# Two weight units of the last expert moved by sixteen transfers of eight rows each

## What is computed

```
def moe_swiglu(h, router_w, w_gate, w_up, w_down):
    logits = (h @ router_w).astype(jnp.float32)
    top_val, top_idx = lax.top_k(logits, TOP_K)
    gates = jax.nn.softmax(top_val, axis=-1)
    ...
    for e in range(N_EXPERTS):
        out = out + gate_dense[..., e:e + 1] * swiglu(h, w_gate[e], w_up[e], w_down[e])
```

## Time and profile before

| | us |
|---|---|
| three runs | 1363.33, 1363.97, 1364.43 |
| their median | 1363.97 |
| the profiled execution | 1363.78 |
| its span | 1361.9 |
| TensorE busy, matmuls | 1296.3 (95%) |
| VectorE busy | 469.0 (34%) |
| ScalarE busy | 341.4 (25%) |
| TensorE waiting for expert weights | 45.3 in 40 waits |

### The profile page before, as it was taken

One profiled execution on the slowest core, in us unless ns is written; L12 is line 12 of the kernel. 1 busy time (PEld: TensorE's weight loads), 2 busy tenths in 40 slices (PEclk: granted clock), 3 DMA queues, 4 the chain that ended last, 5 costly groups with the idle time before them and its releaser, 6 DMA issues.

```text
span 1361.9 us, 31406 instructions
## 1 busy us (share of the span) xinstructions
PE 1296.3 (95%) x14058; PEld 947.3 (70%) x14058; DVE 469.0 (34%) x821; ACT 341.4 (25%) x593; POOL 85.6 (6%) x113
## 2 busy tenths in 40 slices
PE   9999999999999999999987789999999999999875
PEld 9889999999998995467552243366676677558333
DVE  7777776777786662100101101000100100110121
ACT  8666443343377552000100000000000000000011
POOL 1000000000000004101020010001001001001000
PEclk9999999999999999999999999999999999999999
DMA  9316544454433289999999999999999999999993
GB/s 372 109 61 248 208 167 182 186 186 172 170 132 106 98 363 425 413 424 414 427 423 419 427 424 418 424 425 414 428 424 415 427 425 414 426 423 421 419 422 156
DMA packets 46736, 443.91 MB, mean 326 GB/s; under 512 B 6992, under 2 KB 9168, under 8 KB 13328
## 3 DMA queue, kind: packets, MB, share of 16 engines
q1 hardware_dynamic: 40896, 434.15, 77.4%
q0 software_dynamic: 5424, 7.51, 2.0%
q10 hardware_dynamic: 288, 0.29, 0.1%
HBM read 438.20 MB, written 5.93 MB: 326 GB/s over the span
## 4 chain that ended last, share of the span: by engine, by line
PE 78%; DMA 11%; SPq 5%; DVE 3%; ACT 2%; issue 1%; another core or an unknown queue 0%; ACTq 0%; DVEq 0%
PE bank L632 77%; DMA moe_ring<-experts 10%; SPq L458 5%; DVE w_pairs L1425 1%; DMA ring<-stream 1%; PE bank L636 0%; PE bank L730 0%; DVE nmx L1510 0%; ACT scratch L1182 0%; PE bank L736 0%; ACT w_pairs L1104 0%; ACT scratch L1181 0%; ACT sq L1124 0%; ACT scratch L1179 0%; DVE parts L1439 0%
## 5 line engine op out<-in xcount | busy, mean ns | idle before, releaser
L632 PE MATMUL bank<-moe_ring,hT 128*32 128x448 f32 x5376 | 512.6, 539 | 31.0 <-DMA moe_ring<-experts 27.9
L632 PEld LDWEIGHTS bank<-moe_ring,hT 128*32 128x32 f32 x5376 | 251.3, 110 | 288.1 <-issue 181.5
L632 PE MATMUL bank<-parts,w_pairs 128*128 128x272 f32 (+1 forms) x3360 | 427.2, 289 | 1.2 <-DVE w_pairs L1432 0.5
L632 PEld LDWEIGHTS bank<-parts,w_pairs 128*128 128x128 f32 x3360 | 421.7, 188 | 4.7 <-issue 2.8
L632 PE MATMUL bank<-moe_ring,scratch 128*32 128x256 f32 x4704 | 270.9, 383 | 18.6 <-DMA moe_ring<-experts 17.3
L1773 DVE SCALAR_TENSOR_TENSOR hT<-bank,slot_norm,scratch 128x224 f32<-128x224 f32 x96 | 40.6, 423 | 705.9 <-ACT scratch L1334 705.9
L632 PEld LDWEIGHTS bank<-moe_ring,scratch 128*32 128x32 f32 x4704 | 199.8, 111 | 90.3 <-issue 23.3
L1425 DVE TENSOR_TENSOR w_pairs<-ring,w_pairs 128x2048 fp32r<-128x2048 f32 x68 | 154.5, 2287 | 32.2 <-ACT w_pairs L1104 32.1
L1334 ACT ACTIVATE scratch<-bank,norm_now 128x224 f32<-128x224 f32 x96 | 41.2, 447 | 494.7 <-PE bank L632 494.7
L1104 ACT ACTIVATE w_pairs<-ring 128x2048 fp32r<-128x2048 f32 x68 | 129.6, 1912 | 90.1 <-PE bank L632 90.0
L1344 ACT ACTIVATE scratch<-bank,slot_gate 128x256 f32<-128x256 f32 x21 | 9.2, 474 | 242.6 <-PE bank L632 242.6
(11 more groups left out here) (216 smaller groups left out, 490.8 us busy)
## 6 DMA issues: line engine op xcount, KB each, us to landing
moe_ring<-experts SPq DMA_DIRECT2D x192, 1792.0 KB, 42.7
ring<-stream SPq DMA_DIRECT2D x68, 1024.0 KB, 5.1
ring<-stream SPq DMA_DIRECT2D x4, 512.0 KB, 7.4
ring<-stream SPq DMA_DIRECT2D x2, 976.0 KB, 4.7
ring<-stream SPq DMA_DIRECT2D x2, 768.0 KB, 10.5
hT<-h SPq DMA_DIRECT2D x4, 272.0 KB, 5.1
ring<-stream SPq DMA_DIRECT2D x4, 256.0 KB, 4.7
acc_rows<-scratch POOLq DMA_DIRECT2D x1, 1024.0 KB, 5.3
```

Of the source, the lines that this page charges most:

```text
L632: return release(nc.tensor.matmul(dst, lhsT, rhs, start=start, stop=stop), inc, count)
```

## The change

A second set of semaphores is made, one for each of the two units in `SPREAD`, the 2nd and the 6th of an expert (m = 1 and 5). `load_expert` gets a flag `final`. With it, these two units are not moved by one transfer of 128 rows but by sixteen: for each block of 32 partitions and each b of 0 to 3, the eight rows a + b, a + b + 4, ..., a + b + 28. All sixteen raise the unit's own semaphore, to 256 in sum, and the buffer's usual semaphore isn't raised for this unit. Which bytes go to which partition is unchanged. The loop of SyncE over the passes is cut so that the very last pass is issued by a separate call with `final=True`; its number is read from `rounds_sb`. TensorE waits in the last pass for 256 on the new semaphore for these two units, and for the units twelve places later in the same buffers it waits for 16 less on the usual one.

```diff
--- before.py
+++ after.py
@@ -70,6 +70,7 @@
 HSLOTS = 3
 PAIR_AT = (4, 0, 2)
 BIG_UNIT = 3584
+SPREAD = (1, 5)
 MOE_SLOTS = 12
 MOE_FROM = 2048
 
@@ -294,7 +295,7 @@
         bank = [banks[:, i, :] for i in range(8)]
 
         slot_in = [sem(f"slot_in{i}") for i in range(SLOTS)]
-        moe_in = [sem(f"moe_in{i}") for i in range(MOE_SLOTS)]
+        moe_in, spread_in = [sem(f"moe_in{i}") for i in range(MOE_SLOTS)], [sem(f"spread_in{i}") for i in range(len(SPREAD))]
         direct_used, split_hi, split_lo, w_used = sem("direct_used"), sem("split_hi"), sem("split_lo"), sem("w_used")
         af_ready, mixf_ready, mix_hi = sem("af_ready"), sem("mixf_ready"), sem("mix_hi")
         first_in, first_hi, first_lo = [sem(f"first_in{i}") for i in range(4)], sem("first_hi"), sem("first_lo")
@@ -450,28 +451,40 @@
                 elif m == 9:
                     sp.wait_ge(w_used, MOE_SPLIT)
 
-            def load_expert(it, e):
+            def load_expert(it, e, final=False):
                 for m, key in enumerate(MOE_ORDER):
                     if m < MOE_SLOTS:
                         first_lap(m)
                     sp.wait_ge(w_used, it * EXPERT_UNITS + (MOE_SPLIT + m - MOE_SLOTS + 1))
-                    sp.dma_start(moe_slots[m % MOE_SLOTS], experts[e * EXPERT_UNITS + m]).then_inc(moe_in[m % MOE_SLOTS], 16)
-
-            def load_others(r):
-                with sp.Fori(1, EXPERTS) as n:
-                    load_expert(r * EXPERTS + n, sp.value_load(order_sb[0:1, n, :], min_val=1, max_val=EXPERTS - 1))
+                    into, what = moe_slots[m % MOE_SLOTS], experts[e * EXPERT_UNITS + m]
+                    if final and m in SPREAD:
+                        for a in range(0, P, 32):
+                            for b in range(4):
+                                r = slice(a + b, a + 32, 4)
+                                sp.dma_start(into[r, :], what[r, :]).then_inc(spread_in[SPREAD.index(m)], 16)
+                    else:
+                        sp.dma_start(into, what).then_inc(moe_in[m % MOE_SLOTS], 16)
+
+            def ordered(n):
+
+                return sp.value_load(order_sb[0:1, n, :], min_val=1, max_val=EXPERTS - 1)
 
             load_expert(0, 0)
             sp.wait_ge(order_ready, 1)
-            load_others(0)
+            with sp.Fori(1, EXPERTS - 1) as n:
+                load_expert(n, ordered(n))
             sp.wait_ge(rounds_ready, 1)
             rounds = sp.value_load(rounds_sb[0:1, 0:1], min_val=1, max_val=ROUNDS)
             with sp.If(rounds > 1):
-                with sp.Fori(1, rounds) as r:
+                load_expert(EXPERTS - 1, ordered(EXPERTS - 1))
+                for r in range(1, ROUNDS):
                     load_expert(r * EXPERTS, 0)
-                    load_others(r)
+                    with sp.Fori(1, EXPERTS if r < ROUNDS - 1 else EXPERTS - 1) as n:
+                        load_expert(r * EXPERTS + n, ordered(n))
             with sp.Else():
                 sp.nop()
+            last = sp.value_load(rounds_sb[0:1, 1:2], min_val=EXPERTS - 1, max_val=PASSES - 1)
+            load_expert(last, ordered(EXPERTS - 1), final=True)
 
             sp.wait_ge(res_ready, 1)
             sp.dma_start(out[0:P, :], res[:, 0, :]).then_inc(out_stored, 16)
@@ -996,7 +1009,11 @@
                 def arrival(key):
 
                     m = MOE_POS[key]
-                    pe.wait_ge(moe_in[m % MOE_SLOTS], it * (16 * EXPERT_UNITS // MOE_SLOTS) + 16 * (m // MOE_SLOTS + 1))
+                    if last and m in SPREAD:
+                        pe.wait_ge(spread_in[SPREAD.index(m)], 16 * P // 8)
+                    else:
+                        early = last and m - MOE_SLOTS in SPREAD
+                        pe.wait_ge(moe_in[m % MOE_SLOTS], it * (16 * EXPERT_UNITS // MOE_SLOTS) + 16 * (m // MOE_SLOTS + 1 - early))
                     return moe_slots[m % MOE_SLOTS]
 
                 def both(s):
```

## The result

The changed kernel takes 1390.96 us (median of four runs, 1390.32 to 1392.52), the kernel before 1363.69 in the same job (four runs, 1363.33 to 1364.43). The ratio is 1.0199, with an interval of 1.0187 to 1.0211: 27.3 us slower. The prediction was 1359.5 with a range up to 1368.5. The profiled execution took 1390.32 us, its span is 1388.5.

The account below looks back on a forecast made before the run. Bound: arrival of the last expert's last weight unit, at about 1346.5 us. Landing 4.7 us earlier, less 0.3 for completion packets, gives -4.4: 1363.78 - 4.4 = 1359.4, as median 1359.5; range 1358.0 to 1368.5.

Parts of the forecast that it names:

- What bounds the kernel: In the last expert, the arrival of the last weight unit, at about 1346.4 us, sets the end.
- the tail: From TensorE's start on the last unit to the end of the span: 15.4 us, expected to stay the same.
- the rows: An eight-row transfer goes to eight fixed engines, so a moved unit gives those 16 rows each, 8.60 us, the others none.
- The 0.3 us for completion packets: 30 additional transfers bring each of eight engines a completion packet per row; between nothing and perhaps 1 us, taken as 0.3.
- the leaders take the two units: Eight engines ending at 1333.2 (leaders) take both moved units, relieving eight ending near 1346.5 (laggards): last landing 4.7 us earlier.
- Rival (b): The eight engines taken are the late-ending ones, or four of each; they end at 1355.1, total 1372.4; chance 0.08.
- sharing: Engines writing the same eight partitions split 26.7 GB/s; absent from the forecast's sum, up to +3.9 us in one rival.
- rival (a): Write side limits: eight partitions accept 26.7 GB/s, upper rows take twice the time; landing +3.9, total 1367.7; chance 0.38.
- win by rows, lose by sharing: Late engines gain by rows no longer carried exactly what shared partitions cost them, ending at 1346.5 as before.
- The issues: SyncE issues 32 transfers in place of 2, about 16 x 0.37 = 5.9 us a moved unit, adding nothing to the sum.
- rival (d): SyncE is held so long by fuller queues that the last units are issued late: 1366 to 1370; chance 0.04.
- hidden: SyncE's issue time is covered, as a unit lands 39 us after its issue; it would count above some 15 us.

Follow-up runs that it names:

- the last experiment: Loads alone replacing the whole program: transfers of one, two or four rows beside whole units, then 96 units streamed without and with 5200 small matmuls; 1167.46 us.
- the split: The changed kernel with no unit moved by small transfers, only SyncE's cut loop and new waits, against the kernel before: 1364.43 us against 1364.48, ratio 1.0.
- A form measured by itself at 61 GB/s: Eight consecutive rows to a transfer instead of rows four apart: 61 GB/s in loads alone; in the changed kernel 1402.63 us, ratio 1.0282 to the kernel before.

## Why the prediction was wrong, step by step

**What bounds the kernel, the tail, the rows.** Right. The last landing sets the end (1346.5 to 1373.0), and the 15.4 us behind it stayed. A small transfer uses eight engines, 4.3 us of rows for each eight. The 0.3 us for completion packets fits as well: a 4-byte packet lasts 9 ns in the median, and a carrier has thirty more of them.

**The step that failed: "the leaders take the two units".** From one look at start times it was argued that the engines which start first lead and that a transfer of eight rows goes to them; so the forecast let the leaders end at 1341.8 and the laggards at 1337.9. That instruction packets put eight engines behind fits the last experiment. That the eight carriers are the eight leaders was not: two laggards are among them. Rival (b) had "the laggards, or four of each" at a chance of 0.08; since the end waits for the last engine, two are as bad as eight, and that rival's 1372.4, "with sharing more", is the nearest of the forecasts. For those two a moved unit brings eight extra rows, 4.3 us, where the forecast gave laggards 8.6 us back in all.

**The term that was put at nothing: sharing.** The forecast's sum had no price for the upper rows; only rival (a) had one, and it was mis-sized. The rival said that a set of partitions takes one engine's rate, so that a leader's upper rows take twice the time and the laggards end as before. A limit shows (61 GB/s; 430 against 266), but the price is paid by all sixteen engines at once (225 GB/s at a full share), laggards too, including the time in which others write foreign rows. So the exchange "win by rows, lose by sharing" that gave 1367.7 has no gain side for a carrier that lags.

**The sum with these two terms in place.** For one moved unit, a lagging carrier has 4.3 us for the eight extra rows, 4.3 for its eight upper rows at half pace, and 4.3 for its own rows slowed while the six leaders, which are some 13 us ahead, write their upper ones. That is 12.9 us, against 12.8 measured for one unit, and 25.8 for two, against 26.6 in the profiled execution and 27.3 in the medians. The parts by experiment: upper rows 17.65, the extra rows 9.6 (the change less the upper rows alone), the split 0. The packets' lengths price the slowed part by themselves: 19.4 less 1.1 is 18.3 us for an engine, where the reckoning has 17.2 for two units; with 8.6 for the extra rows that makes 26.9. The division into three equal terms is a reckoning that fits; what was measured apart are the halves, the two counts of units and this sum.

**The issues.** Predicted 0.37 us each, hidden. The timeline of SyncE in the changed kernel (start, length, what):

```profile
1206.33 13.59 SPq L464 DMA_DIRECT2D moe_ring<-experts  x16
1220.20 6.62 SPq L466 DMA_DIRECT2D moe_ring<-experts  x3
1227.08 23.35 SPq L464 DMA_DIRECT2D moe_ring<-experts  x16
```

An unhindered one takes 0.65 us and the next starts 0.85 us later: 13.6 us a unit, more than twice the 5.9 of the prediction. The second sixteen were held by full queues on top (23.35). They stand in the chain of waits, which would suggest rival (d). The experiments speak against it: sixteen such issues with lower rows alone cost nothing, and two units cost about twice one unit, although the second's issues took 10 us longer. No run has all 32 issues without the upper rows, so a microsecond or two may still be theirs: 27.3 is 1.7 more than twice 12.8. They may have left the two earliest engines without work for a while, for the share is 0.94 from 1249 to 1256 and these two land the last unit 26 and 23 us later than with lower rows alone; that is behind the others' delay and doesn't set the end. The step "hidden" held in the main, its size did not.

**What the page could not say.** The chain gives 13% to weight transfers and 6% to SyncE, and the busy share of the DMA engines hardly moves (77.4% to 77.2%). The cause is in two other numbers, the rate beside a full share, and a plateau's height divided by one engine's rate.

**What stays open.** Why engines that don't write to the crowded partitions slow down as well. The runs show that they do, not where they wait, nor whether it is the partitions or the rows' places in device memory that count: a run that loads upper source rows into lower partitions would tell. (The Trainium skill, "DMA: Bandwidth & Descriptors", in "Back-pressure in remote DMA", says for transfers between cores that a saturated port stops the path for other engines on it. The 298 GB/s with two such engines would go with that, but these are loads from device memory and no run here tells one path from another.) Open too is which two laggards are among the carriers, since the trace doesn't name the engine of a packet.

None of the runs points to a version that beats the kernel before: the only faster one leaves 1.8 MB out. The laggards' 13 us were not taken off by such transfers, because those go to a fixed set of engines that holds two laggards, and because rows that an engine writes outside its usual partitions slowed the pace of all (225 against 427 GB/s).

## What to carry to other kernels

In these loads, spread over all the DMA engines, each engine has its usual partitions; a transfer cut otherwise can hand it others, and here that slowed every engine (432 to 298 GB/s with two such engines). So test a cut's rate beside whole transfers, in the halves of the partitions separately, before building on it. Read a rate beside its busy share, and divide a final plateau by one engine's rate to count who is late. A gain from rebalancing counts only if no late engine is among those that take the work: here two of the eight carriers were late, and their extra rows (8.6 of some 27 us) fell in full on the end.

## What the runs showed that was not expected

- Two engines with foreign rows slow all sixteen: 432 to 298 GB/s with two-row transfers, 429 to 284 with four, 430 to 266 with eight.
- Beside matmuls that bring 66 instruction packets of 16 KB, eight engines end 12.5 us behind the others, some 1.5 us a packet, where a row of 14,336 bytes takes 0.54; without matmuls all sixteen end within 3 us.
- SyncE's issue of an eight-row transfer takes 0.65 us and comes every 0.85, that of a 128-row one 0.33.
- A form measured by itself at 61 GB/s cost 38.7 us in the kernel, where that rate had given 55 and more.
